# The first feed-forward weight piece fetched and split ahead of the last experts' down projections, in a two-block transformer kernel

## The reference

```python
# end of block 1: 32 experts, 2 of them for each token, hidden width 256
hid = jax.nn.silu(xc @ w_gate[e]) * (xc @ w_up[e])
out = hid @ w_down[e]                                    # then weighted and added to the token's row

# start of block 2: D_FF = 2816
h = rms_norm_2(x, ffn1_norm[l])
x = x + FFN_RESIDUAL_WEIGHT * swiglu(h, ffn1_w_gate[l], ffn1_w_up[l], ffn1_w_down[l])
def swiglu(x, w_gate, w_up, w_down):
    return (jax.nn.silu(x @ w_gate) * (x @ w_up)) @ w_down
```

## Time and profile before

| what | value |
|---|---|
| three timed runs | 1001.49, 1001.91, 1003.04 us |
| median | 1001.91 us |
| profiled execution: device time, span | 1001.2 us, 999.4 us |
| PE busy, share of the span | 976.4 us, 98% |
| DVE busy | 540.9 us, 54% |
| ACT busy | 417.3 us, 42% |
| mean granted TensorE clock | 0.998 |

### The profile page before, as it was taken

How to read it: one execution, slowest core, us unless ns; L and a number is a source line. 1 busy time by engine, 2 the same in 40 slices (tenths; PEclk the granted TensorE clock), 3 DMA queues, 4 the chain that set the end, 5 groups by cost and what they waited for, 6 DMA issues and landing times.

```text
span 999.4 us, 13187 instructions
## 1 busy us (share of the span) xinstructions
PE 976.4 (98%) x5289; PEld 754.0 (75%) x5289; DVE 540.9 (54%) x841; ACT 417.3 (42%) x561; POOL 52.8 (5%) x60
## 2 busy tenths in 40 slices
PE   8999999999999999999999999999999999999997
PEld 7877885653433668888888999877888878888886
DVE  5688561222332175454546595687776664545454
ACT  5565332321221063434344445575643354343442
POOL 3430000000000010000000000000210010000000
PEclk9999999999999999999999999999999999999999
DMA  8965798999999977555555646433275556556541
GB/s 289 323 237 203 302 420 330 421 421 420 421 422 420 410 227 260 182 196 174 204 172 169 220 141 226 140 114 106 88 262 177 170 180 201 188 182 195 174 162 43
DMA packets 97452, 239.59 MB, mean 240 GB/s; under 512 B 7170, under 2 KB 52314, under 8 KB 82042
## 3 DMA queue, kind: packets, MB, share of 16 engines
q1 hardware_dynamic: 95482, 229.57, 63.5%
q0 software_dynamic: 1920, 9.33, 2.7%
HBM read 237.81 MB, written 3.43 MB: 241 GB/s over the span
## 4 chain that ended last, share of the span: by engine, by line
PE 85%; DMA 6%; DVE 4%; SPq 2%; ACT 1%; issue 1%; POOL 0%; ACTq 0%; POOLq 0%; DVEq 0%
PE banks L1264 20%; PE banks L1266 20%; PE banks L1265 20%; PE banks L1618 4%; PE banks L1647 3%; DMA gain_and_spare<-in_w_down 3%; PE banks L1630 3%; DMA conv_room<-in_w_up 3%; PE banks L1321 2%; SPq L530 2%; PE banks L1611 1%; PE banks L1598 1%; PE banks L1470 1%; PE banks L1287 1%; PE banks L1742 1%
## 5 line engine op out<-in xcount | busy, mean ns | idle before, releaser
L2152 DVE TENSOR_TENSOR weights_lo<-raw_weights,weights_hi 128x2048 fp32r<-128x2048 f32 x115 | 263.3, 2290 | 142.0 <-ACT weights_hi L809 141.6
L809 ACT ACTIVATE weights_hi<-raw_weights 128x2048 fp32r<-128x2048 f32 x115 | 219.7, 1913 | 130.5 <-PE banks L1266 113.5
L1264 PE MATMUL banks<-weights_hi,normed_T_hi 128*128 128x512 f32 (+1 forms) x580 | 230.9, 398 | 0.0
L1266 PE MATMUL banks<-weights_hi,normed_T_lo 128*128 128x512 f32 (+1 forms) x580 | 224.9, 388 | 0.0
L1265 PE MATMUL banks<-weights_lo,normed_T_hi 128*128 128x512 f32 (+1 forms) x580 | 224.2, 387 | 0.0
L1264 PEld LDWEIGHTS banks<-weights_hi,normed_T_hi 128*128 128x128 f32 x580 | 109.3, 188 | 23.8 <-issue 3.0
L1266 PEld LDWEIGHTS banks<-weights_hi,normed_T_lo 128*128 128x128 f32 x580 | 108.9, 188 | 22.9
L1265 PEld LDWEIGHTS banks<-weights_lo,normed_T_hi 128*128 128x128 f32 x580 | 109.2, 188 | 19.9
L1264 PE MATMUL banks<-weights_hi,ffn_hidden_T_hi 128*128 128x512 f32 x160 | 62.4, 390 | 0.0
L1266 PE MATMUL banks<-weights_hi,ffn_hidden_T_lo 128*128 128x512 f32 x160 | 62.3, 389 | 0.0
L1265 PE MATMUL banks<-weights_lo,ffn_hidden_T_hi 128*128 128x512 f32 x160 | 62.2, 389 | 0.0
(11 more groups left out here) (425 smaller groups left out, 1701.6 us busy)
## 6 DMA issues: line engine op xcount, KB each, us to landing
raw_weights<-in_w_in SPq DMA_DIRECT2D x37, 1024.0 KB, 5.0
raw_weights<-in_ffn_w_gate SPq DMA_DIRECT2D x44, 512.0 KB, 4.0
raw_weights<-in_ffn_w_up SPq DMA_DIRECT2D x44, 512.0 KB, 5.0
raw_weights<-in_ffn_w_down SPq DMA_DIRECT2D x22, 1024.0 KB, 4.8
stage<-in_w_down SPq DMA_DIRECT2D x12, 1024.0 KB, 22.4
expert_weights<-in_w_up SPq DMA_DIRECT2D x10, 1024.0 KB, 25.1
expert_weights<-in_w_down SPq DMA_DIRECT2D x10, 1024.0 KB, 23.8
expert_weights<-in_w_gate SPq DMA_DIRECT2D x10, 1024.0 KB, 23.5
```

What stands on the lines that cost most here:

```text
L809: ins = eng.activation(w_hi[:, slot, :], raw, ACT.Copy)
L1264: eng.matmul(dst, x[0], w[0], start=first_one, stop=False)
L1266: return eng.matmul(dst, x[1], w[0], start=False, stop=last_one)
L2152: ins = eng.tensor_tensor(w_lo[:, slot, :], raw, w_hi[:, slot, :], ALU.subtract)
```

## The change

Piece 0 is treated apart from pieces 1 and 2. Its two DMAs are issued between the last four experts' sides and their downs, instead of behind the downs. ACT makes its high part ahead of step 12's Silu instead of behind its `rows_out`. DVE makes its rest behind step 12's slot weights instead of in the opening of the feed-forward network. No instruction is added or removed.

```diff
@@ sync @@
                 for e in (2 * j + 10, 2 * j + 11):
                     load_sides(e)
-            eng.wait_ge(ex_down, 2 * STEPS_OF_EXPERTS - 4)
+            load(BEFORE_MOE, True)
             for e in range(LAST_FOUR, EXPERTS):
                 load_down_of(e)
-            for n in range(BEFORE_MOE, BEFORE_MOE + STEPS):
+            for n in range(BEFORE_MOE + 1, BEFORE_MOE + STEPS):
                 load(n, True)
@@ scalar @@
             for j in range(2, STEPS_OF_EXPERTS):
+                if j == STEPS_OF_EXPERTS - 1:
+                    feed(BEFORE_MOE, BEFORE_MOE + 1)
                 hidden_silu(j)
                 if j + 2 < STEPS_OF_EXPERTS:
                     windows_of(j + 2, j % 2).then_inc(window_ready, 1)
                 rows_out(j)
-            feed(BEFORE_MOE, BEFORE_MOE + 1)
@@ vector @@
                 slot_weights(j % 2, ex_selTc)
+                if j == STEPS_OF_EXPERTS - 1:
+                    eng.wait_ge(ex_gu, STEPS_OF_EXPERTS)
+                    feed(BEFORE_MOE, BEFORE_MOE + 1)
                 for x, h in enumerate((1, 0)):
                     eng.wait_ge(ex_hi, j * 2 + (x + 1))
                     rest_of_rows(h, ex_lo)
@@
             t8_half(0, 1)
-            feed(BEFORE_MOE, BEFORE_MOE + 1)
             add_experts(1, 1, first_rows, 2)
             t8_half(0, 0)
```

## The result

The changed kernel takes **1006.01 us** (median of 7 executions, 1003.59 to 1008.04), the kernel before 1002.45 us (7 executions, 1001.26 to 1003.23). The ratio is 1.004, with an interval of 1.003 to 1.0049.

A forecast was written before the change was run, and what follows sets the result against it. PE bounds the kernel (85% of its chain), the last down's landing setting the time at the edit. Queue +3.0, DVE -1.0 and clock +1.2 give +3.2 us on 1001.9: 1005.1 us, range 1002.4 to 1007.5.

The forecast's parts named there:

- The queue term: Full DMA queue: with piece 0 ahead of the four downs, the last down lands later and PE waits, +3.0 us.
- The lower bound of 1.7: Last down's delay computed from bytes and queue rates: it lands 1.7 us later.
- rival 2: At the queue, downs pass piece 0 and land no later; time 1000.9 us, chance 0.08.
- the upper value: Last down's delay taken from the earlier trace, same six transfers in the other order: 3.0 us.
- The moved wait: On the DMA queue, downs waiting for step 11's down matmuls cost nothing beyond the order: 0.
- ACT's high part: ACT's 1.90 us activation for piece 0, moved ahead of step 12's Silu, costs and gains nothing: 0.
- Rival 4: Piece 0 lands too late and ACT's activation delays step 12's Silu; case 1's time plus the excess, chance 0.40 with rival 1.
- DVE's rest: Moving DVE's 2.28 us out of the feed-forward opening brings PE's transposes earlier, -1.0 us, ACT being next in line.
- Rival 3: In the feed-forward opening DVE's full time is won and nothing is lost: 999.7 us, chance 0.04.
- The clock: PE's gap of 4.3 us before step 12's downs lets the clock fall, slowing the down matmuls, +1.2 us.
- Rival 1: The clock holds in PE's gap before step 12's downs: 1003.9 us, chance 0.40 together with rival 4.

The follow-up runs named there:

- e1: The kernel before with only piece 0's two DMAs issued ahead of the last four downs, ACT and DVE work at the old places: 1006.78 us.
- e3: The changed kernel plus 18 filler matmuls on PE, into a bank nobody reads, ahead of step 12's wait for its downs: 1003.90 us.
- e4: The changed kernel with DVE's making of the rest of piece 0 put back to its old place: 1007.37 us.
- e2: The kernel before with only the moved wait: the last four downs wait for step 11's down matmuls instead of step 10's: 1001.78 us.
- e6: The kernel before with pieces 0 to 2 issued only when step 12's gates and ups are done: 1001.82 us.
- e7: The kernel before with the rest of piece 0 made by GpSimd instead of DVE: 1007.49 us.
- e8: The kernel before with piece 0's rest made by GpSimd and pieces 0 to 2 issued only after step 12's gates and ups: 1007.07 us.
- e9: The kernel before, transfer order kept; piece 0's gate half gets its own semaphore and is converted early on ACT and DVE: 1000.79 us.
- e10: As e9, and ACT makes piece 1's high part ahead of tile 0's first `t8_half`: 1001.09 us.
- e5: The kernel before with only piece 0's gate half (512 KB) issued ahead of the last four downs, the up half behind: 1004.31 us.

## Why the prediction was right, and where it was off

I forecast 1005.1 us in a range of 1002.4 to 1007.5, and slower. Measured are 1006.01 us, 3.6 to 4.2 us more than before, where the sum was +3.2.

- **The queue term, +3.0: right.** The four profiles with the whole piece ahead (after, e1, e3, e4) have the last down at 155.5 to 157.1 us after step 2's Silu, mean 156.1. The seven with the downs ahead (before, e2, e6, e7, e8, e9, e10) have it at 152.6 to 153.3, mean 152.9. The difference is 3.2 us, or 2.9 without the change's own profile, whose last side is already 1.3 us late, and half a piece (e5) gives 1.2. The lower bound of 1.7 and rival 2 (the downs land no later) fall. What spoke for rival 2, the gate half landing together with the last down, doesn't hold where the half has its own semaphore: it lands 1.5 us behind (e9, e10).
- **The reason I gave for taking the upper value: wrong.** I said that the last down loses 1.3 us to the small packets behind it. e6 held piece 0's back until 2.7 us before the landing and e2 left them, and both have 10.5 us from the last side to the last down; e8 held them back and e7 left them, and both have 11.4. A small remainder isn't excluded by that. In the kernel before these were 11.3 us, and the side landed earlier there than in e2 and e6 (141.3 us after step 2's Silu, 142.4 and 142.6 in those two). The upper value held because it was a measured time for the same six transfers, not because of that mechanism.
- **The moved wait, 0: right** (e2: ratio 1.0; 417 GB/s in the change from 325 to 338).
- **ACT's high part, 0: right.** It ended 2.70 us before the Silu's input was ready. Rival 4 falls.
- **DVE's rest, -1.0: right.** 9.45 us became 8.42 in the change and in e3, and it was 9.4 in e1 and e4, where the rest stands at its old place. The next in line was ACT, as said. Rival 3 falls.
- **The clock, +1.2: the right mechanism, too small a size.** PE's gap was 4.6 us (forecast 4.3), and the downs took 1.47 us longer in the change, 1.70 in e1 and 2.72 in e4, mean 2.0. e3, which differs from the change in the fillers alone, is 2.1 us faster on the medians. I had taken 1.2 with nothing but "nearer to the lower end" behind it. The clock stayed low for 3.4 us in the change and in e1 and for 6.8 us in e4, and no row of before could tell that. One reading behind the term was wrong: the wait of 1.8 us in the earlier trace rows is the first 1.76 us of the span, neither at work nor at full clock. The record reads 1.00 there, but the 20 fillers behind it take 4.64 us, 0.23 each, and twelve of the same take 1.50 us, 0.13 each, from 8.90 on. No term hung on it. With 3.2 for the queue and 2.0 for the clock the sum is +4.2.
- **Rival 1, the clock holds: not the likely case.** It gave 1003.9. e3, where the clock holds at this place, measured 1003.90. Of the change's seven executions one, with 1003.59 us, may be of that kind. Its mean granted clock (0.999) doesn't settle it: e3's profile has a mean of 0.996 and holds the clock here, its low stretches being the opening and the end.

The moment of the fall was told from one row, 3.0 us after the last matmul. At work it came 3.1 us (e4), 4.1 us (after) and 5.0 us (e1) after it, in the other gap 2.5 us (e7) and 3.5 us (e8), and around the 2.9 us of e5's gap it didn't come. The Trainium skill (TensorE: Matmul & The Clock Gate, "What's actually happening"), cited in the prediction, says that the monitor doesn't start anew with the kernel and that the moment of a change of the clock varies for this reason. These runs agree as far as they go: each moment is one profile of another kernel, but e7 and e8 have the same matmuls and the same wait (4.13 and 4.14 us) and fell 1.0 us apart.

What stays open: why e5's median is 1.0 us above what the queue term gives, and the 1.3 us by which the change's profiled execution is late between step 2 and the last side, ahead of the first edit.

## What to carry to other kernels

When a queue is full and PE waits for its last transfer, a piece put ahead costs its whole transfer time (3.2 us here), however early its consumer could use it; look which landing PE waits for before moving anything in front of it. To win the early conversion, move the conversion alone, on the half that has landed (e9_halves), and leave the order of the transfers; here that is 1.0 us in the profile and not yet clear of the noise in time. A wait of PE that grows from 1 to 4 us must be priced with the clock too: here that was a third of what the transfers' order lost (1.70 of 4.9 us in e1).

## What the runs showed of the hardware

- The granted clock needs no long idleness to fall: in gaps of 4.1 to 4.6 us at work it fell in every profile without fillers (after, e1, e4, e7, e8; in e1 0.5 us behind the gap), 2.5 to 5.0 us after the last matmul. Behind the gaps of 4.4 to 4.6 us the 32 matmuls took 1.5 to 2.7 us longer. Some 4 us of fillers in the gap kept it at 1.00 (e3).
- No shorter gap is shown to be safe. At the edited place nothing fell around gaps of up to 2.9 us, but in the kernel's opening four profiles (e1, e2, e3, e7) show a fall to 0.50 within 1.1 us of the end of waits of 1.9 to 2.4 us.
- A DVE operation of 0.69 us took 5.02 us beside a GpSimd subtraction of 4.49 us. An idle GpSimd was no free place for the 2.28 us of DVE's work.
- A down issued 8.4 us later (7.5 counted from step 2's Silu) landed within 0.4 us of before (e2): 21.6 us on its way instead of 28.7. In a full queue the time from issue to landing says how much lies ahead, not how fast a transfer is.
